# Sparse stages of a 12-stage transformer kernel: next stage's first weight item split between the last two units, and the first two units' outputs taken before the third unit's maximum

## The chip, the cores and the metric

The kernel runs on one core of a Trainium2 chip. The metric is the device time of one execution in microseconds (us). Engines are named as in the profile: PE is TensorE (matmuls; PEld are its weight loads), DVE is VectorE, ACT is ScalarE, POOL is GpSimd, SP is SyncE, which issues the weight transfers. All engines run their own instruction streams and wait for each other on semaphores.

## What is computed

Two blocks, each of depth 2, over 256 tokens of width 1024, in fp32. The first block has feed-forward, a hybrid mixer, cross-attention to a memory and a second feed-forward; the second block, which is where the change is, has a mixer with sparse attention and a squared-relu feed-forward. Cut to the part that matters:

```python
def second_block(x, positions, ...):
    for l in range(DEPTH):                                # DEPTH = 2
        h = rms_norm_2(x, g_pre_mix[l])
        u_pool, q, k, v, iq, ik, iw = split(h @ w_in[l])  # q, k, v: 512 wide, 8 heads of 64
        ...                                               # rotary positions
        a_out = pool_mixer(u_pool, w_pool[l], pool_scale[l])
        b_out = dsa_attention(q, k, v, iq, ik, iw, 64)    # 64 best keys per query by an index score
        mix = concatenate([a_out, b_out]) @ w_out[l]
        x = x + rms_norm_2(mix, g_post_mix[l])
        h = rms_norm_2(x, g_pre_ffn[l])
        f = square(relu(h @ w_ff1[l])) @ w_ff2[l]         # 1024 -> 4096 -> 1024
        x = x + rms_norm_2(f, g_post_ffn[l])
# in dsa_attention, for the chosen keys of each query:
#   s = q . k / 8 ; p = softmax(s) ; o = p @ v
```

## The kernel before

The work is a row of 12 stages, numbered s = 0 to 11: ffn, hybrid, memory, ffn, twice, then sparse, relu, sparse, relu. The two sparse stages are s = 8 and s = 10; each is followed by a relu stage (9 and 11). The order of the work is written out by hand, once for each engine (functions `scalar`, `vector`, `tensor`, `gpsimd`, `sync`); nothing reorders it. On DVE and ACT every instruction waits for the one before it on the same engine.

Weights come in items of 1 MB (mostly 128 x 2048 elements). SP loads item i into one of four `raw` buffers once DVE has finished item i - 4. Each item is then split in two numbers of lower precision that TensorE multiplies: ACT writes the high part (`whi`, or `mhi` where the fourth home is used), DVE the low part, raw minus high (`wlo` or `mlo`), each in two halves of 128 x 1024. `split_to(i, halves)` on either engine advances this splitting up to item i (with `halves=1`, to its first half only), and `take(s, tag, c)` means `split_to` of that item plus AHEAD = 2: two items ahead of the one that PE works on. ACT may write an item's high part only when PE has finished with the item that had the same home (the event `used`). For the first item of a relu stage that older item is `w_out2` number 2. So in a sparse stage `take(s, "w_out2", 2)` is the splitting of the first item of the *next* stage, called `ff1 0` in this text, and `take(s, "w_out2", 3)` that of the second, `ff1 1`.

Activations are split in the same way: PE transposes a tile of 128 tokens (`blocks`), ACT writes the high part into `ahl`, DVE the low part (`halves` on both engines). PE's product with that tile waits for DVE's part.

Attention of a sparse stage is done in four units u = 0 to 3 (tokens tile 0 with head groups 0 and 1, then tile 1 with the same). For each unit PE makes the scores; DVE adds the mask, takes the maximum and negates it (`head(u)`: two additions from PSUM, a reduction, a small multiplication); ACT takes exponentials with their sums (`exps`); PE transposes them (`turn_scores`); ACT, and for units 2 and 3 DVE too, copy them back (`turned`); PE multiplies with the values (`values`); DVE divides by the sums into XN (`out(u)`: a reciprocal and a multiplication). PE transposes XN's half (`blocks`) for the output product `out_part`. `out_part(x, m)` is item x of `w_out2` times tokens tile m: 12 matmuls. PE's order at the end of the stage is `out_part(2,0)`, `turn_scores(2)`, `out_part(2,1)`, `values(2)`, `turn_scores(3)`, `out_part(3,0)`, `values(3)`, `out_part(3,1)` with the last transposition in it, `out_part(0,1)`, `out_part(1,1)` with the transpositions of the next stage's tokens, and then the product that opens the next stage, which begins with `ff1 0`.

At the same place DVE's order is: `turned(2)`, `out(2)`, `turned(3)`, `weigh` and `renew` (which norm tile 0's result and add it to the running X), `out(3)` between them, `halves` of the last tile, then the splitting of `ff1 0` and `ff1 1`, and then the next stage's `halves(s, 0, 0, 0)`, which its first product needs. ACT's is: exponentials of unit 3, `turned(3)`, the squares of tile 0's result (`post_square`), the splitting of `ff1 0`, `halves` of the last tile, `ff1 1`.

Of the kernel before, what the change touches and what calls it, by code (L numbers as in the profile page):

```python
# [32 lines left out]
AHEAD = 2  # L33
# [107 lines left out]
def bm(ap, n):  # L141
    return ap.unsqueeze(1).broadcast_to([ap.shape[0], n, ap.shape[1]])
# [120 lines left out]
def build(nc, A, out):  # L263
    ctx = ExitStack()
    with ctx:
# [178 lines left out]
        number = {x[0]: i for i, x in enumerate(items)}  # L444
# [239 lines left out]
        def scalar(e):  # L684
# [23 lines left out]
            def take(s, tag, c, ahead=AHEAD):  # L708
                split_to(number[s, tag, c] + ahead)
# [142 lines left out]
            def exps(name, l, u, w, P, scale):  # L852
                n, d = (snb, sden) if name == "s" else (nb, den)
                o = 4 * (u if name == "s" else u % 2)
                q.wait_ge(*dve.at(name + "_max", l, u))
                for i in range(4):
                    put(P[u % 2][:, i, 0:w], P[u % 2][:, i, 0:w], ACT.Exp, (name + "_exp", l, u, i), scale=scale,
                        bias=n[:, o + i:o + i + 1], accum_out=d[:, o + i:o + i + 1])
# [149 lines left out]
            def sparse(s):  # L1008
                l = STAGES[s][1]

                def natural(banks, o, name):
                    q.wait_ge(*pe.at(name, l))
                    for m in range(2):
                        put(o[:, m * 512:(m + 1) * 512], PS[:, banks[m], :], ACT.Copy, (name, l) if m else (name, l, 0),
                            scale=r2[:, m:m + 1])

                def heads(o, bank, name):
                    for m in range(2):
                        q.wait_ge(*pe.at(name, l, m))
                        put(o[:, :, m * 128:(m + 1) * 128], PS[:, bank + m, :].rearrange("p (k n) -> p k n", k=4), ACT.Copy,  # L1020
                            (name, l, m))

                def index(m):
                    q.wait_ge(*pe.at("index", l, m))
                    put(RL[m], PS[:, 4:8, :].rearrange("p b (a n) -> p b a n", a=2)[:, :, :, 0:128 * (m + 1)], ACT.Relu,
                        ("index", l, m), scale=0.125 * 8.0 ** -0.5)

                def turned(u):
                    q.wait_ge(*pe.at("s_turned", l, u, 0))
                    put(sPT[u % 2][:, 0:512], PS[:, STURN[u][0], :], ACT.Copy, ("s_pt", l, u))  # L1030

                for m in range(2):
                    q.wait_ge(*pe.at("first", s, m))
                    q.wait_ge(*pool.at("r2", s, m))
                    put(iqk[:, m, 0:292], PS[:, m, 0:292], ACT.Copy, ("iq_first", l, m), scale=r2[:, m:m + 1])
                    put(iqk[:, m, 292:576], PS[:, 4 + m, 0:284], ACT.Copy, ("iq_rest", l, m), scale=r2[:, m:m + 1])
                for m in range(2):
                    put(iw[:, m, :], PS[:, 4 + m, 284:292], ACT.Copy, ("iq", l) if m else ("iw", l), scale=r2[:, m:m + 1])
                for c in range(2):
                    take(s, "q", c)  # L1040
                natural((2, 3), qn, "q")
                heads(iqT, 4, "iqT")
                for c in range(2):
                    take(s, "k", c)
                index(0)
                take(s, "v", 0)
                natural((0, 1), kn, "k")
                index(1)
                q.wait_ge(*dve.at("score", l, 0))
                heads(sqT, 2, "sqT")  # L1050
                take(s, "v", 1)
                heads(skT, 2, "skT")
                take(s, "u", 0)
                natural((0, 1), V, "v")
                exps("s", l, 0, 128, sP, 1.0)
                exps("s", l, 1, 128, sP, 1.0)
                turned(0)
                turned(1)
                take(s, "u", 1)
                take(s, "w_out2", 0)  # L1060
                natural((2, 3), U, "u")
                halves(s + 0.5, 0, 1, TILEBANK[0])
                for a in range(2):
                    q.wait_ge(*pe.at("means", l, a))
                    put(DT[:, a * 512:a * 512 + 512], PS[:, MEANBANK[a], :], ACT.Copy, ("means", l, a))
                exps("s", l, 2, 256, sP, 1.0)
                for a in range(2):
                    q.wait_ge(*pe.at("pooled", l, a))
                    for g in (2 * a, 2 * a + 1):
                        put(ahv[:, g, :], PS[:, POOLBANK[a], (g % 2) * 256:(g % 2) * 256 + 256], ACT.Copy,  # L1070
                            ("pooled", l, g), scale=PSC[:, l * 4 + g:l * 4 + g + 1])
                take(s, "w_out2", 1)
                turned(2)
                exps("s", l, 3, 256, sP, 1.0)
                turned(3)
                post_square(s + 1, 0)
                take(s, "w_out2", 2)
                halves(s + 0.5, 1, 1, TILEBANK[1])
                take(s, "w_out2", 3)

# [6 lines left out]
        def vector(e):  # L1087
# [27 lines left out]
            def split_to(i, halves=2):  # L1115

                while at["split"] < 2 * min(i, len(items) - 1) + halves:
                    n, h = at["split"] // 2, at["split"] % 2
                    at["split"] += 1
                    k, w = items[n][2:4]  # L1120
                    raw, (hi, lo) = raw_of(n), homes[place[n]]
                    c = slice(h * k * w // 2, (h + 1) * k * w // 2)
                    q.wait_ge(*act.at("hi", n, h))
                    tt(lo[:, c], raw[:, c], hi[:, c].bitcast(F32), ALU.subtract, *([("lo", n)] if h else []))

            def take(s, tag, c, ahead=AHEAD):
                split_to(number[s, tag, c] + ahead)
# [54 lines left out]
            def weigh(s, m):  # L1182

                if m == 0:
                    post_weigh(s, m, 0)
                post_var(s, m)
                post_weigh(s, m, 1)
# [378 lines left out]
            def sparse(s):  # L1566
# [26 lines left out]
                def head(u):  # L1593
                    m, g = SUNITS[u]
                    w, b = 128 * (m + 1), SBANK[u]
                    bi = PSC2[:, m * 128:m * 128 + w]
                    q.wait_ge(*pe.at("s_scores", l, u))
                    if u >= 2:
                        q.wait_ge(*pe.at("s_turned", l, u - 2, SUNITS[u - 2][0]))
                    for i in range(2):  # L1600
                        sv = PS[:, b + i, :].rearrange("p (a n) -> p a n", a=2)[:, :, 0:w]
                        stt(sP[u % 2][:, 2 * i:2 * i + 2, 0:w], sv, 0.125, bm(bi, 2), ALU.mult, ALU.add, ("s_shift", l, u, i))
                    o = 4 * u
                    red(smx[:, o:o + 4], sP[u % 2][:, :, 0:w], ALU.max)
                    ts(snb[:, o:o + 4], smx[:, o:o + 4], -1.0, None, ALU.mult, ALU.bypass, ("s_max", l, u))

                def turned(u):
                    q.wait_ge(*pe.at("s_turned", l, u, 1))
                    cp(sPT[u % 2][:, 512:1024], PS[:, STURN[u][1], :], ("s_pt", l, u))

                def out(u):
                    m, g = SUNITS[u]
                    o = 4 * u
                    q.wait_ge(*act.at("s_exp", l, u, 3))
                    rcp(sden[:, o:o + 4], sden[:, o:o + 4])
                    x0 = m * DM + 512 + g * 256

                    q.wait_ge(*pe.at("s_values", l, 1 if u == 0 else u))
                    tt(XN[:, x0:x0 + 256].rearrange("p (a b d) -> p b a d", a=2, b=2),
                       PS[:, SVALUE[u], (u % 2) * 256:(u % 2 + 1) * 256].rearrange("p (b a d) -> p b a d", b=2, a=2),  # L1620
                       bc(sden[:, o:o + 4].rearrange("p (b a) -> p b a", a=2), 64), ALU.mult, ("s_out", l, u))
# [6 lines left out]
                head(0)  # L1628
                head(1)
                select(1)  # L1630
                head(2)
                out(0)
                out(1)
                take(s, "u", 0)
                halves(s + 0.5, 0, 1, TILEBANK[0])
                take(s, "u", 1)
# [6 lines left out]
                head(3)  # L1643
                take(s, "w_out2", 1)
                turned(2)
                out(2)
                turned(3)
                weigh(s + 1, 0)
                out(3)
                renew(s + 1, 0, (0,))  # L1650
                halves(s + 0.5, 1, 1, TILEBANK[1])
                renew(s + 1, 0, (1,))
                take(s, "w_out2", 2)
                take(s, "w_out2", 3)

            for s in range(12):
# [685 lines left out]
```

## Time and profile before

| | |
|---|---|
| time, median of 3 runs | 1870.56 us (1870.31 to 1873.33) |
| profiled execution | 1871.79 us, of which the span from first to last instruction is 1869.7 us |
| granted TensorE clock, mean | 1.000 |
| PE matmuls busy | 1840.9 us, 98% of the span |
| DVE busy | 1314.5 us, 70% |
| ACT busy | 1042.5 us, 56% |
| POOL busy | 216.6 us, 12% |
| DMA | 339.46 MB, mean 182 GB/s |

The profile gives busy times by engine, the waits between engines, and a timeline of each engine. A timeline's row has the start from the span's beginning, the duration, the engine, the line of the helper that issued the instruction, what it writes and reads, the count of merged instructions, and in brackets how long the engine sat idle before it and which engine's result ended that. Since helpers issue nearly everything, most rows have the same few line numbers: 1667 for PE's matmuls, 1672 for its transpositions, 1093 for DVE's two-operand operations, 690 for everything on ACT; one tells them apart by the tile names and by their place.

### The profile page before, as it was taken

What the parts mean: (1) busy time and instruction counts of PE and PEld (TensorE: products, weight loads), DVE (VectorE), ACT (ScalarE), POOL (GpSimd) and SP (SyncE); (2) the same over time, 40 slices, a digit from 0 to 9 for tenths busy, and PEclk for the clock granted to TensorE, in tenths of its full rate; (3) what the DMA queues carried; (4) which work ended last, traced back from release to release, by engine and by line L of the source; (5) the groups of instructions that cost most, each with busy time, mean ns of one, the idle gap of its engine ahead of it and who ended that gap; (6) DMA issues with size and microseconds to landing.
All of it is one profiled execution on the core that took longest, in us unless ns stands there. A gap on an engine that the chain in (4) does not pass through costs nothing.

```text
span 1869.7 us, 27904 instructions
## 1 busy us (share of the span) xinstructions
PE 1840.9 (98%) x10911; PEld 1609.9 (86%) x10911; DVE 1314.5 (70%) x1734; ACT 1042.5 (56%) x1503; POOL 216.6 (12%) x264
## 2 busy tenths in 40 slices
PE   6999999999999999999999999999999999999998
PEld 6888899888888888889998988888888888888887
DVE  5776758777766776676687677666887667787665
ACT  4655545655655565555456566555755545665453
POOL 1010101010100011001021000002201111301110
PEclk9999999999999999999999999999999999999999
DMA  8585663355566556766344536655546654636562
GB/s 288 180 300 188 169 201 121 113 176 174 181 202 203 180 182 233 258 169 223 124 136 136 169 136 225 202 178 168 180 135 205 197 184 164 225 96 210 180 198 73
DMA packets 229971, 339.46 MB, mean 182 GB/s; under 512 B 22278, under 2 KB 178064, under 8 KB 229840
## 3 DMA queue, kind: packets, MB, share of 16 engines
q1 hardware_dynamic: 221968, 307.91, 50.2%
q0 software_dynamic: 7872, 29.78, 4.8%
q8 instruction: 85, 1.39, 0.3%
q14 instruction: 46, 0.38, 0.1%
HBM read 336.62 MB, written 1.05 MB: 181 GB/s over the span
## 4 chain that ended last, share of the span: by engine, by line
PE 90%; DVE 7%; ACT 2%; issue 1%; DMA 1%; DVEq 0%; SPq 0%; ACTq 0%
PE ps L1667 87%; PE ps L1672 3%; DVE wlo L1093 2%; ACT region L690 1%; DVE xn L1093 1%; DVE region L1101 1%; DVE mlo L1093 1%; DMA raw<-ffn_w_gate 1%; DVE xs L1101 1%; ACT whi L690 1%; DVE ahl L1093 0%; DVE hlo L1093 0%; DVE region L1093 0%; DVE region L1590 0%; DVE sm L1588 0%
## 5 line engine op out<-in xcount | busy, mean ns | idle before, releaser
L1093 DVE TENSOR_TENSOR wlo<-raw,whi 128x1024 fp32r<-128x1024 f32 (+2 forms) x458 | 559.5, 1222 | 178.1 <-ACT whi L690 143.6
L690 ACT ACTIVATE whi<-raw 128x1024 fp32r<-128x1024 f32 (+2 forms) x458 | 482.5, 1053 | 66.9 <-PE ps L1667 15.9
L1667 PE MATMUL ps<-ahl,whi 128*128 128x512 f32 (+1 forms) x1920 | 433.4, 353 | 0.2
L1667 PEld LDWEIGHTS ps<-ahl,whi 128*128 128x128 f32 x1920 | 331.2, 190 | 43.1 <-DVE hlo L1093 0.9
L690 ACT ACTIVATE region<-ps 128x512 f32<-128x512 f32 (+2 forms) x260 | 150.2, 578 | 335.8 <-PE ps L1667 251.2
L1667 PE MATMUL ps<-whi,ahl 128*128 128x512 f32 (+2 forms) x1120 | 303.5, 348 | 9.2 <-DVE ahl L1093 8.8
L1667 PE MATMUL ps<-ahl,wlo 128*128 128x256 f32 x1568 | 269.1, 282 | 0.0
L1667 PEld LDWEIGHTS ps<-ahl,wlo 128*128 128x128 f32 x1568 | 233.3, 191 | 11.9
L1667 PEld LDWEIGHTS ps<-whi,ahl 128*128 128x128 f32 x1120 | 197.6, 190 | 35.0 <-DVE ahl L1093 10.9
L1093 DVE TENSOR_TENSOR mlo<-raw,mhi 128x1024 fp32r<-128x1024 f32 x130 | 160.8, 1237 | 49.8 <-ACT mhi L690 40.8
L1667 PE MATMUL ps<-wlo,ahl 128*128 128x512 f32 (+2 forms) x560 | 191.4, 342 | 0.0
L1667 PE MATMUL ps<-whi,hhi 128*128 128x512 f32 x472 | 185.7, 394 | 2.0 <-DVE hlo L1093 2.0
L1667 PE MATMUL ps<-wlo,hhi 128*128 128x512 f32 x472 | 184.3, 390 | 0.0
L1667 PE MATMUL ps<-whi,hlo 128*128 128x512 f32 x472 | 183.8, 389 | 0.0
L531 POOL TENSOR_TENSOR hlo<-region,hhi 128x512 fp32r<-128x512 f32 x62 | 81.1, 1308 | 798.8 <-ACT hhi L690 798.8
L690 ACT ACTIVATE mhi<-raw 128x1024 fp32r<-128x1024 f32 x130 | 137.5, 1058 | 12.9 <-PE ps L1667 5.1
L1667 PE MATMUL ps<-ahl,mhi 128*128 128x512 f32 (+1 forms) x640 | 144.5, 354 | 0.1
L1093 DVE TENSOR_TENSOR region<-region,ps 128x512 f32<-128x512 f32 x102 | 70.1, 688 | 96.3 <-ACT region L690 90.1
L1667 PE MATMUL ps<-region 128*128 128x64 f32 (+5 forms) x928 | 130.1, 327 | 0.0
L690 ACT ACTIVATE hhi<-region 128x512 fp32r<-128x512 f32 x68 | 43.0, 632 | 150.0 <-DVE region L1101 76.6
L1667 PEld LDWEIGHTS ps<-region 128*128 128x128 f32 (+2 forms) x928 | 109.3, 179 | 16.7 <-issue 3.5
L1667 PEld LDWEIGHTS ps<-ahl,mhi 128*128 128x128 f32 x640 | 110.8, 190 | 14.6 <-DVE hlo L1093 0.3
(166 smaller groups left out, 2379.8 us busy)
## 6 DMA issues: line engine op xcount, KB each, us to landing
raw<-w_ff SPq DMA_DIRECT2D x64, 1024.0 KB, 5.4
raw<-ffn_w_gate SPq DMA_DIRECT2D x44, 1024.0 KB, 5.3
raw<-ffn_w_up SPq DMA_DIRECT2D x44, 1024.0 KB, 5.7
raw<-ffn_w_down SPq DMA_DIRECT2D x44, 1024.0 KB, 5.0
raw<-w_in SPq DMA_DIRECT2D x38, 1024.0 KB, 6.1
raw<-w_out SPq DMA_DIRECT2D x16, 1024.0 KB, 4.9
raw<-xa_wk SPq DMA_DIRECT2D x8, 1024.0 KB, 5.2
raw<-xa_wv SPq DMA_DIRECT2D x8, 1024.0 KB, 5.0
```

The lines of the kernel that those rows point to most:

```text
L531: e.tensor_tensor(o, a, b, op).then_inc(*pool.did(*names))
L690: e.activation(o, i, f, **kw).then_inc(*act.did(*names))
L1093: e.tensor_tensor(o, a, b, op).then_inc(*dve.did(*names))
L1101: e.scalar_tensor_tensor(o, a, s, b, op0, op1).then_inc(*dve.did(*names))
L1667: m = e.matmul(o, l, r, start=start, stop=stop)
L1672: m = e.transpose(o, i, CS[0:k, 0:k])
```

## The change

Four edits, all in the sparse stages, in the orders of DVE and ACT. PE's, POOL's and SP's orders are as before.

```diff
@@ scalar: sparse @@
                 take(s, "w_out2", 1)
                 turned(2)
                 exps("s", l, 3, 256, sP, 1.0)
+                take(s, "w_out2", 2)
                 turned(3)
                 post_square(s + 1, 0)
-                take(s, "w_out2", 2)
                 halves(s + 0.5, 1, 1, TILEBANK[1])
                 take(s, "w_out2", 3)
@@ vector: sparse @@
                 head(0)
                 head(1)
                 select(1)
-                head(2)
                 out(0)
                 out(1)
+                head(2)
                 take(s, "u", 0)
                 halves(s + 0.5, 0, 1, TILEBANK[0])
                 take(s, "u", 1)
@@ vector: sparse @@
                 head(3)
                 take(s, "w_out2", 1)
                 turned(2)
+                split_to(number[s, "w_out2", 2] + AHEAD, halves=1)
                 out(2)
                 turned(3)
+                take(s, "w_out2", 2)
                 weigh(s + 1, 0)
                 out(3)
                 renew(s + 1, 0, (0,))
                 halves(s + 0.5, 1, 1, TILEBANK[1])
                 renew(s + 1, 0, (1,))
-                take(s, "w_out2", 2)
                 take(s, "w_out2", 3)
```

On DVE, after the selection of the 64 keys of tile 1 in stage 8 (the `pc` row is its end), the order before (-) and after (+); `small` holds maxima and sums, `xn` rows are `out(0)` and `out(1)`:

```order
 L1097 TENSOR_SCALAR pc<-region 128x256
-L1101 SCALAR_TENSOR_TENSOR region<-ps,pc 128x512 x2
-L1109 TENSOR_REDUCE small<-region 128x4
-L1097 TENSOR_SCALAR small<-small 128x4
 L1113 RECIPROCAL small<-small 128x4
 L1093 TENSOR_TENSOR xn<-ps,small 128x2x2x64
 L1113 RECIPROCAL small<-small 128x4
 L1093 TENSOR_TENSOR xn<-ps,small 128x2x2x64
+L1101 SCALAR_TENSOR_TENSOR region<-ps,pc 128x512 x2
+L1109 TENSOR_REDUCE small<-region 128x4
+L1097 TENSOR_SCALAR small<-small 128x4
 L1093 TENSOR_TENSOR wlo<-raw,whi 128x1024 x2
```

The four instructions of `head(2)` moved behind the four of the two outputs.

On DVE at the end of stage 8, from the last weight item before `turned(2)` on; the `mlo` rows are the halves of `ff1 0`:

```order
 L1093 TENSOR_TENSOR wlo<-raw,whi 128x1024 x2
 L1105 COPY region<-ps 128x512
+L1093 TENSOR_TENSOR mlo<-raw,mhi 128x1024
 L1113 RECIPROCAL small<-small 128x4
 L1093 TENSOR_TENSOR xn<-ps,small 128x2x2x64
 L1105 COPY region<-ps 128x512
+L1093 TENSOR_TENSOR mlo<-raw,mhi 128x1024
 L1093 TENSOR_TENSOR xn<-ps,gv 128x512
 L1097 TENSOR_SCALAR nm<-nm 128x1
```

One half now stands ahead of `out(2)`, the other behind the copy of `turned(3)`; further down, between `renew` and the pair of `ff1 1`, both are gone (in stage 10 the same, with `wlo` in place of `mlo`):

```order
 L1101 SCALAR_TENSOR_TENSOR xs<-xn,nm,xs 128x512
 L1093 TENSOR_TENSOR xn<-xs,gv 128x512
-L1093 TENSOR_TENSOR mlo<-raw,mhi 128x1024 x2
 L1093 TENSOR_TENSOR wlo<-raw,whi 128x1024 x2
 L1093 TENSOR_TENSOR ahl<-ps,ahl 128x4x128
```

What is left behind them is the pair of `ff1 1` and then the next stage's first `halves`.

On ACT in stage 8, from the exponentials of unit 3 on:

```order
 L690 ACTIVATE region,small<-region,small 128x256 x4
-L690 ACTIVATE region<-ps 128x512
-L690 ACTIVATE region,nm<-ps 128x512 x2
-L690 ACTIVATE mhi<-raw 128x1024 x2
+L690 ACTIVATE mhi<-raw 128x1024 x2
+L690 ACTIVATE region<-ps 128x512
+L690 ACTIVATE region,nm<-ps 128x512 x2
 L690 ACTIVATE ahl<-ps 128x4x128
```

The high part of `ff1 0` moved from behind the copy of `turned(3)` and the two squares to ahead of them.

## Rows read from the trace of the kernel before

**Rows 1.** Waits of PE, 1280 to 1400 us: total, times, longest
```profile
PE ps L1667 <- DVE ahl L1093: 1.6, 2, 0.9
```
**Rows 2.** Timeline of PE: start, duration, what, count, idle before
```profile
1377.41 0.39 PE L1667 MATMUL ps<-mhi,ahl 128*128 128x512 f32 x1
...
1394.38 0.39 PE L1667 MATMUL ps<-wlo,ahl 128*128 128x512 f32 x1
1394.61 0.40 PE L1667 MATMUL ps<-whi,ahl 128*128 128x512 f32 x1
1395.90 0.36 PE L1667 MATMUL ps<-mhi,ahl 128*128 128x256 f32 x1 [0.90 <-DVE ahl L1093]
...
1396.93 0.40 PE L1667 MATMUL ps<-mhi,ahl 128*128 128x256 f32 x2
...
1397.29 0.50 PE L1667 MATMUL ps<-mhi,ahl 128*128 128x256 f32 x2
...
1683.92 0.35 PE L1667 MATMUL ps<-whi,ahl 128*128 128x256 f32 x1 [0.90 <-DVE ahl L1093]
```
**Rows 3.** Timeline of PE's weight loads
```profile
1360.58 0.42 PEld L1672 LDWEIGHTS ps<-cs,xn 128*128 128x128 f32 x4 [0.53 <-DVE xn L1093]
...
1363.89 0.19 PEld L1667 LDWEIGHTS ps<-whi,ahl 128*128 128x128 f32 x1 [0.23 <-DVE ahl L1093]
...
1386.09 0.59 PEld L1672 LDWEIGHTS ps<-cs,xn 128*128 128x128 f32 x4
...
1395.87 0.19 PEld L1667 LDWEIGHTS ps<-mhi,ahl 128*128 128x128 f32 x1 [1.31 <-DVE ahl L1093]
```
**Rows 4.** Timeline of DVE, end of stage 8 and start of 9
```profile
1376.86 0.69 DVE L1105 COPY region<-ps 128x512 f32<-128x512 f32 x1
...
1379.70 0.42 DVE L1093 TENSOR_TENSOR xn<-ps,small 128x256 f32<-128x256 f32 x1 [1.94 <-PE ps L1667]
1380.58 0.69 DVE L1105 COPY region<-ps 128x512 f32<-128x512 f32 x1 [0.46 <-PE ps L1672]
1382.75 0.69 DVE L1093 TENSOR_TENSOR xn<-ps,gv 128x512 f32<-128x512 f32 x1 [1.48 <-ACT region L690]
1384.06 0.21 DVE L1097 TENSOR_SCALAR nm<-nm 128x1 f32<-128x1 f32 x1 [0.62 <-ACT region L690]
...
1385.32 0.42 DVE L1093 TENSOR_TENSOR xn<-ps,small 128x256 f32<-128x256 f32 x1
...
1389.82 2.48 DVE L1093 TENSOR_TENSOR mlo<-raw,mhi 128x1024 fp32r<-128x1024 f32 x2
1392.41 2.55 DVE L1093 TENSOR_TENSOR wlo<-raw,whi 128x1024 fp32r<-128x1024 f32 x2
1395.07 0.69 DVE L1093 TENSOR_TENSOR ahl<-ps,ahl 128x512 fp32r<-128x512 f32 x1
```
**Rows 5.** Timeline of ACT, same stretch
```profile
1377.67 0.19 ACT L690 ACTIVATION_READ_ACCUMULATOR region<-region,small 128x1 f32 x1
1380.15 0.60 ACT L690 ACTIVATE region<-ps 128x512 f32<-128x512 f32 x1 [2.29 <-PE ps L1672]
...
1384.12 2.15 ACT L690 ACTIVATE mhi<-raw 128x1024 fp32r<-128x1024 f32 x2
...
1392.52 0.60 ACT L690 ACTIVATE ahl<-ps 128x512 fp32r<-128x512 f32 x1 [1.97 <-PE ps L1672]
...
1394.34 0.60 ACT L690 ACTIVATE ahl<-ps 128x512 fp32r<-128x512 f32 x1 [0.44 <-PE ps L1672]
```
**Rows 6.** Timeline of DVE, middle of stage 8
```profile
1355.93 1.42 DVE L1101 SCALAR_TENSOR_TENSOR region<-ps,pc 128x512 f32<-128x512 f32 x2
...
1363.15 0.69 DVE L1093 TENSOR_TENSOR ahl<-ps,ahl 128x512 fp32r<-128x512 f32 x1
```
**Rows 7.** Timeline of SP, stage 8; page: weight transfers, KB each, us to landing
```profile
1363.07 54.59 SPq L501 DMA_DIRECT2D raw<-w_ff  x9
```
```profile
raw<-w_ff SPq DMA_DIRECT2D x64, 1024.0 KB, 5.4
```

## The prediction

> **What bounds the kernel now.** I read the page's busy times first: PE is busy for 1840.9 of 1869.7 us, 98%, as the small table has it. PE's own order is untouched, so an edit on DVE or ACT can only give back a stretch in which PE waits for them, or make a new one. The second view is therefore PE's waits around the first sparse stage and its end [rows 1]: 1.6 us in two waits, both for DVE's low part of the activations (`ahl`), the longest 0.9. The third is PE's timeline, for where that wait stands: at 1395.90, the first matmul of stage 9, whose left operand is `mhi`, that is `ff1 0`; stage 11 has its twin at 1683.92, also 0.90 [rows 2]. The other wait of [rows 1] lies ahead of the edited code, at the start of stage 8, and is left alone.
>
> What is DVE doing while PE waits? The fourth view, DVE's timeline, shows the low part at 1395.07, ended 0.69 later at 1395.76, with PE following 0.14 behind. Straight ahead of it stand two pairs of weight halves, `mlo` (`ff1 0`, 2.48 us) from 1389.82 and `wlo` (`ff1 1`, 2.55) from 1392.41 [rows 4]. ACT had written the high part of the same activations at 1392.52 + 0.60 = 1393.12 [rows 5]. So for 1.95 us the low part could have been made and was queued behind weights. A little earlier DVE sits idle for 1.94, 0.46, 1.48 and 0.62 us [rows 4].
>
> **Part 1: the halves of ff1 0 move forward.** First whether they fit.
>
> ACT: its exponentials end at 1377.67 + 0.19 = 1377.86, and it then idles 2.29 us until 1380.15, when it copies unit 3 [rows 5]. Its pair of high halves costs 2.15 [rows 5]. They may start when `w_out2` 2 is used, which is PE's last matmul of `out_part(2,1)`, 1377.41 + 0.39 = 1377.80 [rows 2]: no wait to speak of. The item itself is in `raw` long since: the first transfer of this stretch of `w_ff` was issued at 1363.07, and such a transfer takes 5.4 us, so 1368.5 [rows 7]. With a few hundredths between instructions the pair runs from about 1377.93 to 1380.10, and the copy at 1380.15 starts 0 to 0.05 late. What is behind it on ACT, the squares, waits for PE anyway.
>
> DVE: the copy of `turned(2)` ends at 1377.55. The first low half waits for ACT's first high half (1377.93 + 1.07 = 1379.00), takes 1.24 (half of 2.48), ends about 1380.27. Queued behind this wait are the reciprocal, the multiplication of `out(2)` and the copy of unit 3. The multiplication, before at 1379.70, comes at about 1380.57, and the copy, before at 1380.58, at about 1381.02: 0.9 and 0.45 us late. Nobody on PE wants `out(2)` at once (its reader is the transposition at 1386.09 [rows 3]); the copy ends at 1381.71, while PE still has `out_part(3,0)` to do before `values(3)`. The second half then takes 1381.80 to 1383.05, in the 1.48 us of idleness before 1382.75, and pushes that instruction by 0.35 to 1383.10. It ends at 1383.80, and the next, at 1384.06, was waiting for ACT with 0.62 of idleness, so it starts on time [rows 4]. From there everything to 1389.78 is as before. The margin: 0.25 us at 1384.06, and behind it another 0.35, since `out(3)` ends at 1385.32 + 0.42 = 1385.74 [rows 4] and PE loads it at 1386.09 [rows 3]. Some 0.6 us in all, and the moved work costs nothing on the path.
>
> What it gives: at 1389.82 the `mlo` pair is gone and DVE goes to `ff1 1`, whose pair ends near 1392.4 instead of 1394.96. ACT's high part at 1393.12 becomes what is late next, and DVE's low part runs from 1393.17 to 1393.86 in place of 1395.76. PE's last matmul before the wait starts at 1394.61 and has 512 columns; it and the one before (1394.38) are 0.23 us apart, so the first of stage 9 would start at 1394.84 instead of 1395.90: 1.06 us, a little more than the 0.90 that the row calls idle and less than the 1.31 of its weight load [rows 2, 3]. Then there is a small second one: in the run of matmuls of 256 columns a pair takes 0.40, but 0.50 at 1397.29 [rows 2], where the second half of the activations is first read. It also goes, since ACT has its high part at 1394.34 + 0.60 = 1394.94 [rows 5] and DVE's low part can follow by 1395.7, while PE would want it at 1394.84 + 1.44 = 1396.3. So 0.10 more, 1.16 us for a sparse stage. Behind that, the chain over tile 1 starts from ACT and DVE work that is earlier by more than 1.16, or from PE, so it moves along, and stages 9 and 11 show PE without a wait in the stretches behind these. Price between bounds: at least the 0.90 of the row if a matmul there starts no sooner, at most the 1.31 of the weight load plus 0.10 = 1.41. I take 1.16.
>
> There is a rule that speaks against the edit. On ACT and DVE each instruction waits for its predecessor, so a half at the head that waits for `used` or for its high part holds back all behind it; in this trace DVE idled 1.94 us for one such wait [rows 4]. The Trainium skill says the same of the queues (TensorE: Matmul & The Clock Gate, the table at its head and "Architectural detail: the array is 16x 32x32, not 1x 128x128"): ACT's and DVE's queues are strictly first in, first out, while PE may pull weight loads ahead. By that rule nothing passes the two halves, and the sum stands only while they fit, which is the rival "slower" below. The second half of the rule, loads pulled ahead, agrees with the trace as far as the load at 1395.87 waited longer (1.31) than its matmul (0.90) [rows 2, 3].
>
> SP: the load of the item four behind `ff1 0` waits for its low part and so is issued about 9 us earlier (1383.1 instead of 1392.3). PE waited for no weights there, so this gives nothing and needs nothing.
>
> **Part 2: out(0) and out(1) ahead of head(2).** It moves two reciprocals and two multiplications forward past four instructions. PE's transposition of them waited 0.53 us at 1360.58 [rows 3]; that wait goes. But DVE is busy without a gap worth naming from 1355.93 to the low part that starts at 1363.15 and ends at 1363.84 [rows 6], and PE's weight load at 1363.89 waits for just that, with 0.23 of idleness [rows 3]. The same instructions stand between, in another order, so it ends at 1363.84 again. PE gets there up to 0.5 earlier and waits that much longer. I price it at 0, bounds +0.1 to -0.3 for a stage: small gaps between dependent small instructions can fall otherwise, and DVE is what decides. `head(2)` ends under 2 us later, and ACT's exponentials of unit 2 stand behind copies of what PE makes after its transposition at 1360.58, which is cover.
>
> **Sum.** Two sparse stages at 1.16 is 2.32 us. The profiled execution took 1871.79, so it would take 1869.47. That execution is 1.23 above the median of the runs shown, 1870.56; on the median the forecast is 1868.24, say 1868.2.
>
> **Rivals.**
> - *The wait is filled, but something else holds PE there* (the low part made in time, then PE stopped by the weights of `ff1 1` or by the second half of the activations). For it: DVE's order is dense there, and `ff1 1` also waits for ACT. Against: by the times above each has 0.6 us or more of margin. It would give about half, 1.2 us: 1869.4. With both gains lost, 1870.6.
> - *Part 2 pays too.* If DVE's stretch to 1363.84 shortens or PE profits from earlier transpositions elsewhere: 0.5 us a stage on top, 1867.2. Against it is the row at 1363.89.
> - *Slower.* The first low half holds `out(2)`, the copy of unit 3 and the post-norm chain. It decides once it is more than 0.6 us late beyond my times, for instance if ACT's high half started late; from there PE loses one for one at 1386.09. To lose on balance it must be over 1.76 us late. Were it late by a whole transfer, 5.4 us [rows 7], the stage would lose 5.4 - 0.6 - 1.16 = 3.6, and the kernel 7.3: 1877.9. Against it: the item lands 9 us before ACT now wants it, and the other release, at 1377.80, is a matmul that PE reaches without help from the moved work.
> - *The change does not do what it says*: the DVE halves land elsewhere. The order shows them where the diff puts them; no chance worth a number of its own.
>
> **How the numbers follow.** Forecast (1.8 to 2.8 us gained) 0.68; gain partly or wholly refilled 0.17; part 2 pays too 0.11; slower 0.04. A measurement of this kernel tells about 0.2% from no change, 3.7 us: faster means below 1866.8, slower above 1874.3. The forecast lies inside. Below 1866.8 I see part of the rival in which part 2 pays, and a forecast that the median of a few runs moves by 1.4 us (the three shown span 3): 0.13. Above 1874.3: 0.04. The rest, 0.83, is within. The range is 1866.5 to 1870.7: from the upper bounds of both parts (1.41 + 0.3 twice, 1867.1, and a little for the runs) to no gain at all.
>
> **What would show it.** Right: no wait of 0.9 us at the first `ff1 0` matmul of stages 9 and 11, each span from the last `out_part` to it shorter by 1.06; DVE's first low half at about 1379.0 with a wait for ACT before it, the second before the post-norm multiplication; that one's successor still at 1384.06; the low part of the activations at about 1393.2, waiting for ACT. For part 2: the wait of 0.53 gone, the one for `ahl` after it grown by as much. Wrong: PE's transposition at 1386.09 later, a wait at `values(3)`, or a new PE wait in the first 15 us of stage 9.

## The result and the profile after

The changed kernel takes 1868.77 us (median of 21 runs, 1867.67 to 1871.5) where the kernel before, timed beside it, takes 1871.36 (21 runs): a ratio of 0.9986, 95% interval 0.9980 to 0.9992, that is 2.6 us faster. Forecast were 1868.2 us and a gain of 2.3 us. The gain is small, below the 3.7 us that the prediction took as what a measurement tells, but with 21 runs each the interval excludes 1: it stands for a gain of 1.5 to 3.7 us.

The profiled execution has a span of 1867.6 us, 2.1 less than before. That understates the edit. PE's first transposition came 0.8 us later in this execution, before any changed instruction, and the delay was still 0.85 us at A in stage 8. So I measure inside the stage, between PE's transpositions, which all kernels of this study have in the same order. For stage 8 in the trace of before they start at: A 1349.83 (exponentials of units 0 and 1), B 1360.58 (the outputs of units 0 and 1), C 1386.31 (the last tile), D 1393.71 (the second of the two transpositions of the next stage's first tokens), E 1408.15 (the scales, near the end of stage 9's first product). The changed kernel's rows are

```profile
1350.68 1.04 PE L1673 MATMUL ps<-cs,region 128*128 128x128 f32 x8
...
1361.24 0.66 PE L1673 MATMUL ps<-cs,xn 128*128 128x128 f32 x4
...
1386.93 0.60 PE L1673 MATMUL ps<-cs,xn 128*128 128x128 f32 x4
...
1394.31 0.60 PE L1673 MATMUL ps<-cs,xn 128*128 128x128 f32 x4
...
1407.44 0.38 PE L1673 MATMUL ps<-cs,nm 128*128 128x128 f32 x2
```

The table is worked out from such starts (us).

| | A to B, stage 8 / 10 | B to C | C to D | D to E | A to E, both stages |
|---|---|---|---|---|---|
| before | 10.75 / 10.58 | 25.73 / 25.72 | 7.40 / 7.40 | 14.44 / 14.44 | 116.46 |
| changed | 10.56 / 10.56 | 25.69 / 25.70 | 7.38 / 7.38 | 13.13 / 13.13 | 113.53 |

The two stretches together are 2.93 us shorter: 2.62 of it is D to E (1.31 us in each), where [rows 2] had the wait, 0.21 is A to B, and 0.10 is B to D. PE's timeline of the changed kernel, from the last `out_part` into the first product:

```profile
1393.86 0.39 PE L1668 MATMUL ps<-wlo,ahl 128*128 128x512 f32 x1
...
1395.21 0.40 PE L1668 MATMUL ps<-whi,ahl 128*128 128x512 f32 x1
1395.45 0.28 PE L1668 MATMUL ps<-mhi,ahl 128*128 128x256 f32 x1
1395.57 0.28 PE L1668 MATMUL ps<-mlo,ahl 128*128 128x256 f32 x1
...
1396.75 0.40 PE L1668 MATMUL ps<-mhi,ahl 128*128 128x256 f32 x2
...
1399.39 0.60 PE L1673 MATMUL ps<-cs,xn 128*128 128x128 f32 x4
```

The first `mhi` matmul follows at 0.24 us, where it was 1.29 later before (1394.61 to 1395.90), and it has no bracket: PE waits for nothing. All pairs are 0.40 long, none 0.50 as in [rows 2].

DVE in the same stretch, the lines that answer to [rows 4]:

```profile
1377.48 0.69 DVE L1105 COPY region<-ps 128x512 f32<-128x512 f32 x1
1379.69 1.23 DVE L1093 TENSOR_TENSOR mlo<-raw,mhi 128x1024 fp32r<-128x1024 f32 x1 [1.52 <-ACT mhi L690]
...
1381.76 0.69 DVE L1105 COPY region<-ps 128x512 f32<-128x512 f32 x1
1382.56 1.23 DVE L1093 TENSOR_TENSOR mlo<-raw,mhi 128x1024 fp32r<-128x1024 f32 x1
1383.91 0.69 DVE L1093 TENSOR_TENSOR xn<-ps,gv 128x512 f32<-128x512 f32 x1
1384.71 0.21 DVE L1097 TENSOR_SCALAR nm<-nm 128x1 f32<-128x1 f32 x1
...
1388.20 0.69 DVE L1093 TENSOR_TENSOR ahl<-ps,ahl 128x512 fp32r<-128x512 f32 x1
...
1390.51 2.55 DVE L1093 TENSOR_TENSOR wlo<-raw,whi 128x1024 fp32r<-128x1024 f32 x2
1393.76 0.69 DVE L1093 TENSOR_TENSOR ahl<-ps,ahl 128x512 fp32r<-128x512 f32 x1 [0.69 <-ACT ahl L690]
```

All times here are 0.62 later than on the scale of [rows 4], by PE's transposition C. The halves are where the forecast put them: the first at 1379.07 on the old scale (forecast 1379.00), the second at 1381.94 (1381.80). The low part of the new tile starts at 1393.14 (forecast 1393.17) and now waits for ACT instead of standing behind weights. Note also what has vanished: the post-norm multiplication at 1383.91 and its successor at 1384.71 have no idle time before them any more, and neither has the low part of the last tile at 1388.20. From 1379.69 to there DVE is one unbroken chain.

ACT answers to [rows 5]:

```profile
1378.60 2.15 ACT L690 ACTIVATE mhi<-raw 128x1024 fp32r<-128x1024 f32 x2
1380.84 0.60 ACT L690 ACTIVATE region<-ps 128x512 f32<-128x512 f32 x1
...
1393.13 0.60 ACT L690 ACTIVATE ahl<-ps 128x512 fp32r<-128x512 f32 x1 [1.96 <-PE ps L1673]
```

The pair fills the old idleness of 2.29 us, and the copy of unit 3 is 0.07 us late by the old scale.

Part 2 shows in DVE's middle stretch (compare [rows 6]) and in the weight loads (compare [rows 3]):

```profile
1358.27 1.42 DVE L1101 SCALAR_TENSOR_TENSOR region<-ps,pc 128x512 f32<-128x512 f32 x2
...
1363.76 0.69 DVE L1093 TENSOR_TENSOR ahl<-ps,ahl 128x512 fp32r<-128x512 f32 x1
```
```profile
1361.23 0.42 PEld L1673 LDWEIGHTS ps<-cs,xn 128*128 128x128 f32 x4 [0.33 <-DVE small L1097]
...
1388.95 0.19 PEld L1668 LDWEIGHTS ps<-whi,ahl 128*128 128x128 f32 x1 [0.46 <-DVE ahl L1093]
```

PE's load of the outputs has 0.33 of idleness left of 0.53, and the load of `out_part(0,0)` behind it, which waited 0.23, is no longer among the rows with a wait. The bracket names the end of `head(2)`, but that is only what ended last before the load. The transposition needs `out(1)`, and that had been done for 3 us; what PE was still at was its own matmuls of unit 3's scores:

```profile
1357.81 0.42 DVE L1093 TENSOR_TENSOR xn<-ps,small 128x256 f32<-128x256 f32 x1
...
1360.17 1.13 PE L1668 MATMUL ps<-region 64*128 64x256 f32 x8
```

From A to B is 10.56 us in both stages now. So the part of the 0.53 that DVE caused was about 0.2.

The row at 1388.95 is the wait for the last tile's low part. It was there in the kernel before as well, and DVE had a little idleness before that part:

```profile
1388.33 0.19 PEld L1667 LDWEIGHTS ps<-whi,ahl 128*128 128x128 f32 x1 [0.45 <-DVE ahl L1093]
```
```profile
1387.58 0.69 DVE L1093 TENSOR_TENSOR ahl<-ps,ahl 128x512 fp32r<-128x512 f32 x1 [0.18 <-ACT ahl L690]
```

### The profile page after: what moved, and what is told of

It is laid out like the page before. It is cut to its first block, busy times and chain, and to the rows that moved or that the text cites. A ratio compares the mean times of both kernels' runs of the same rounds, so it can differ in the third digit from the quotient of the medians.

```text
span 1867.6 us, 27904 instructions
## 1 busy us (share of the span) xinstructions
PE 1840.6 (99%) x10911; PEld 1611.5 (86%) x10911; DVE 1314.9 (70%) x1734; ACT 1042.3 (56%) x1503; POOL 216.3 (12%) x264
## 3 DMA queue, kind: packets, MB, share of 16 engines
HBM read 336.62 MB, written 1.05 MB: 181 GB/s over the span
## 4 chain that ended last, share of the span: by engine, by line
PE 92%; DVE 5%; ACT 2%; DMA 1%; issue 1%; DVEq 0%; SPq 0%; ACTq 0%
PE ps L1668 89%; PE ps L1673 3%; DVE wlo L1093 2%; ACT region L690 1%; DVE xn L1093 1%; DMA raw<-ffn_w_gate 1%; DVE region L1101 1%; DVE mlo L1093 1%; ACT whi L690 1%; DVE xs L1101 0%; DVE hlo L1093 0%; DVE ahl L1093 0%; DVE region L1093 0%; ACT hhi L690 0%; ACT mhi L690 0%
```

## The experiments

In each, the ratio is to the kernel before timed beside it, and A to E is the sum of both stages, to be compared with 116.46 (before) and 113.53 (changed).

**Halves only.** `out(0)` and `out(1)` put back behind `head(2)`:

```diff
-                out(0)
-                out(1)
                 head(2)
+                out(0)
+                out(1)
```

> Only the halves of ff1 0 moved (ACT and DVE), the two outputs left behind head(2). Theory: nearly all of the change is here. PE's stretch from the last transposition of stage 8 to the first of the next product loses about 1.3 us a stage (1.06 of the wait, the rest small waits behind it), in all 2.6 us against the kernel before; DVE's stretch from the key selection to the low part of tile 0 stays as long as before (7.61 and 7.44 us in the trace before). Rival (the two edits need each other): less than 1.5 us in all.

Measured: 1869.64 us, ratio 0.9988 (0.9979 to 0.9997). A to E 113.89, so 2.57 less than before; D to E 13.13 in both stages, as in the changed kernel. A to B 10.77 and 10.59, as before. The theory holds: the moved halves are nearly all of the gain.

**Outputs first only.** The kernel before with `out(0)`, `out(1)` ahead of `head(2)`, the halves untouched.

> Only out(0) and out(1) ahead of head(2). Theory as predicted: 0, since DVE decides at the low part of tile 0. What the changed kernel's trace says instead: DVE's stretch from the selection to that low part is 7.37 us in both sparse stages, where it was 7.61 and 7.44, so PE gains what DVE's stretch loses, 0.24 and 0.07 us, 0.3 in all. Rival (part 2 pays by itself as much as its wait): 0.5 us a stage, 1.0 in all.

Measured: 1871.35 us, ratio 0.9999 (0.9990 to 1.0008): a run cannot tell it from nothing. The trace can: A to E 116.21, 0.25 less, nearly all in A to B (10.56 in both stages). DVE shows where it comes from. The kernel before and, second, this one, from the second reciprocal:

```profile
1359.72 0.18 DVE L1113 RECIPROCAL small<-small 128x4 f32<-128x4 f32 x1
1360.10 0.42 DVE L1093 TENSOR_TENSOR xn<-ps,small 128x256 f32<-128x256 f32 x1 [0.21 <-DVE small L1113]
```
```profile
1356.21 0.18 DVE L1113 RECIPROCAL small<-small 128x4 f32<-128x4 f32 x1
1356.42 0.42 DVE L1093 TENSOR_TENSOR xn<-ps,small 128x256 f32<-128x256 f32 x1
```

The multiplication starts 0.20 behind its reciprocal's end in the first, 0.03 in the second. That gap stands at this place in stage 8 in all three traces with the old order (before, halves only, and ACT only, below) and in none of the nine with the new one; in stage 10 the old order does not have it. The rest of what DVE's stretch lost in stage 8 (7.61 to 7.37 us, from the selection's last instruction to the low part), 0.07, is shorter gaps elsewhere. Stage 10 is the control: its old order has no such gap, DVE's stretch went from 7.44 to 7.37 us, and PE gained 0.02 from A to B and 0.04 in all. So moving the outputs forward gained next to nothing by itself; what PE gained in stage 8 is what the gap had cost. The two parts together should give 2.57 + 0.25 = 2.82; the changed kernel has 2.93.

**One half.** DVE's second half of `ff1 0` left at its old place:

```diff
                 turned(3)
-                take(s, "w_out2", 2)
                 weigh(s + 1, 0)
 ...
                 renew(s + 1, 0, (1,))
+                take(s, "w_out2", 2)
                 take(s, "w_out2", 3)
```

> The changed kernel, but DVE's second half of ff1 0 left where it was before; only the first half goes ahead of out(2). Theory (PE waits for the low part of the activations behind whatever stands before it, until ACT's high part decides): with one half left, the low part starts 1.24 us earlier than before, at 1393.8 on the time scale of before, and ends at 1394.5, just before PE's weight load at 1394.6. So the large wait of 1.06 still goes, but the small ones behind it come back in part: 1.0 to 1.2 us a stage instead of 1.3. Rival (a half counts as a half): 0.65 us a stage.

Measured: 1869.32 us, ratio 0.9987 (0.9978 to 0.9996). D to E 13.20 in both stages: a gain of 1.24 from the first half, and 0.07 more from the second. A wait behind two pieces of 1.24 us is not halved when one leaves: the one was enough to put the low part ahead of PE. Expected were 1.0 to 1.2, a little low; the rival's 0.65 is out.

**Unsplit.** Both halves ahead of `out(2)`:

```diff
-                split_to(number[s, "w_out2", 2] + AHEAD, halves=1)
+                take(s, "w_out2", 2)
                 out(2)
                 turned(3)
-                take(s, "w_out2", 2)
```

> The changed kernel, but both halves of ff1 0 on DVE ahead of out(2), so not split between the units. Theory (0.6 us of margin): the copy of unit 3 ends 1.24 + 0.1 us later than in the changed kernel, on the changed kernel's time scale at about 1383.8, where PE's weight load for values(3) starts at about 1383.5: PE loses 0.2 to 0.4 us a stage there; behind it nothing else, so the kernel is 0.4 to 0.8 us slower than the changed one. Rival (splitting does not matter): same within 0.1 us. Rival (splitting is what pays): 2.5 us slower.

Measured: 1869.29 us, ratio 0.9988 (0.9980 to 0.9997); A to E 114.00, 0.47 more than the changed kernel. B to C is 25.90 and 25.93 where the changed kernel has 25.69 and 25.70, and nothing else differs by more than 0.02. So splitting the item between the units is worth 0.2 us a stage, at the low end of what was expected; runs cannot tell it.

**ACT only.** The kernel before with ACT's `take` moved and nothing on DVE.

> The kernel before, with only ACT's part of the move: its high halves of ff1 0 come ahead of the copy of unit 3, DVE's order is that of before. Theory (DVE's queue makes the wait, not ACT's): DVE's low part of the activations starts where it did, the waits of 0.90 us at the first matmul of stages 9 and 11 stay, the time is that of before within 0.2 us. Rival (ACT's late high half was what held DVE): the wait goes and the kernel gains 1 us or more a stage.

Measured: 1871.99 us, ratio 1.0002 (0.9993 to 1.0011), A to E 116.51, D to E 14.44 and 14.46. DVE's order makes the wait; ACT's move only allows DVE's.

**DVE only.** The changed kernel with ACT's `take` back behind `post_square`.

> The changed kernel, with ACT's high halves left where they were. This is the forecast's slower rival made real: DVE's first low half must wait for ACT's high half, which comes 6.2 us later than in the changed kernel, and out(2), the copy of unit 3 and the norm chain are queued behind it. Theory (0.6 us of margin at the end, about 1.2 us at values(3), then one for one): DVE's first half starts at 1385.2 on the time scale of before, the copy of unit 3 ends at about 1387.9, where PE wants it at 1382.9, so PE waits about 5 us at values(3) in stages 8 and 10; gained back is the 1.2 to 1.3 us of the later wait. Net 3.5 to 4 us slower a stage, 7 to 8 us in all against before. Rival (PE has other work to cover it): under 2 us.

Measured: 1885.2 us (4 runs), ratio 1.0071 (1.0056 to 1.0086): 13.5 us slower, nearly twice what was expected. DVE, then PE:

```profile
1385.34 1.23 DVE L1093 TENSOR_TENSOR mlo<-raw,mhi 128x1024 fp32r<-128x1024 f32 x1 [7.66 <-ACT mhi L690]
...
1387.40 0.69 DVE L1105 COPY region<-ps 128x512 f32<-128x512 f32 x1
```
```profile
1383.04 0.39 PE L1668 MATMUL ps<-whi,ahl 128*128 128x512 f32 x1
1388.24 3.64 PE L1668 MATMUL ps<-region 128*128 128x64 f32 x16 [4.82 <-DVE region L1105]
1391.65 0.77 PE L1668 MATMUL ps<-whi,ahl 128*128 128x512 f32 x1
1392.22 0.63 PE L1668 MATMUL ps<-wlo,ahl 128*128 128x512 f32 x1
```

The wait is as forecast: DVE's half at 1385.34, the copy ended at 1388.09, PE 4.82 us idle at `values(3)`. But the 16 matmuls of `values(3)` then take 3.64 us instead of 1.89 (changed kernel), and those behind them 0.63 instead of 0.39. The stage by stretches (columns: length, busy us and instructions of PE, PEld, DVE, ACT, POOL, then the granted clock, DMA share, GB/s):

```profile
1384.00:1388.00 4.00, 0.00 (x0) 0.00 (x0) 2.42 (x4) 2.27 (x4) 0.00 (x0) 0.92 0.00 0
1388.00:1390.00 2.00, 1.75 (x9) 1.79 (x9) 1.79 (x3) 0.00 (x0) 0.00 (x0) 0.50 0.00 0
1390.00:1392.00 2.00, 2.00 (x10) 2.00 (x10) 1.38 (x5) 0.00 (x0) 0.56 (x1) 0.50 0.65 141
1392.00:1394.00 2.00, 2.00 (x6) 1.52 (x6) 1.78 (x3) 0.00 (x0) 0.00 (x0) 0.50 1.04 368
1394.00:1396.00 2.00, 2.00 (x12) 1.53 (x10) 0.47 (x2) 0.60 (x1) 0.00 (x0) 0.96 0.05 15
```

The granted clock falls in the last part of the wait (a mean of 0.92 over the first row), is 0.50, the lower level of 1.2 GHz, until about 1394, and then full again. B to C grew by 33.53 - 25.69 = 7.84 us against the changed kernel: 5.20 - 0.23 = 4.97 from the last matmul before the wait to the first after it, and 6.04 - 3.17 = 2.87 from there to C, which is the clock.

In stage 10 PE is idle as long (4.81, the 16 matmuls 3.65 long), but the lower level lasts longer, from the wait until about 1691, past C at 1688.85:

```profile
1688.00:1690.00 2.00, 2.00 (x8) 1.70 (x7) 0.51 (x1) 0.06 (x1) 0.00 (x0) 0.50 0.26 93
1690.00:1692.00 2.00, 2.00 (x8) 1.53 (x8) 1.40 (x2) 0.54 (x2) 0.00 (x0) 0.72 0.00 0
```

There B to C grew by 7.92 and C to D by 0.78, so the same wait cost 7.8 us in one stage and 8.7 in the other. The two waits alone, 4.97 and 4.96, less the 2.93 of the changed kernel, would be 7.0 us against the kernel before, as expected; the clock is the rest.

The Trainium skill (TensorE: Matmul & The Clock Gate, "Part 1: The HAM clock gate") says that an idle TensorE falls to its lower clock and has to earn the higher one back; the trace agrees, with the 0.50 above while PE was busy again.

**Extra half.** The changed kernel, with the first half of `ff1 0` computed once more between the copy of unit 3 and the second half:

```diff
                 out(2)
                 turned(3)
+                again(number[s, "w_out2", 2] + AHEAD)   # lo[:, first half] = raw - hi
                 take(s, "w_out2", 2)
```

> The changed kernel with one more half on DVE: the first low half of ff1 0 is computed a second time, between the copy of unit 3 and the second half (1.24 us with its gap about 1.3; the result is the same). Theory: it eats the margin and what is over moves PE one for one. In the changed kernel's trace the norm's multiplication had ended 0.1 us before its successor started, out(3) ends at 1386.39 and PE's load of it is at about 1386.7. With 1.3 us more, less the 0.1 and the 0.3, PE loses about 0.9 to 1.0 us a stage, 1.8 to 2.0 us against the changed kernel. Rival (DVE's idle time of 70% busy covers it): 0. Rival (a DVE instruction on this stretch always counts in full): 2.6 us.

Measured: 1871.29 us, ratio 0.9997 (0.9989 to 1.0006). A to E 115.96, 2.43 more than the changed kernel: 1.21 a stage. Neither the expected 0.9 to 1.0 nor the rival's 1.3 is met, and the rival is nearer. B to C grew by 0.78 and 0.76, about as the theory has it (PE waits for `out(3)`), but C to D by 0.44 and 0.45, which it did not have. PE:

```profile
1387.19 0.66 PE L1679 MATMUL ps<-cs,xn 128*128 128x128 f32 x4 [0.61 <-DVE xn L1093]
...
1389.65 0.50 PE L1674 MATMUL ps<-whi,ahl 128*128 128x512 f32 x1 [0.41 <-DVE ahl L1093]
```

**Extra half, tile first.** To find what the second wait is:

```diff
                 out(3)
-                renew(s + 1, 0, (0,))
                 halves(s + 0.5, 1, 1, TILEBANK[1])
+                renew(s + 1, 0, (0,))
                 renew(s + 1, 0, (1,))
```

> The kernel with the extra half, with one more edit on DVE: the low part of the last tile (`halves` of 8.5 and 10.5) goes ahead of the first half of `renew`. The extra half alone cost 1.21 us a stage, of which 0.78 at the last transposition (PE waits for out(3)) and 0.44 behind it, up to out_part(0,1). New theory: that 0.44 is DVE's queue again, since the low part stood behind renew's two instructions, which the extra half had made later; taken out of it, the stretch from the last transposition to the second of the next tokens returns from 7.82 to 7.38 us, while the 0.78 stay: 0.43 us a stage back. Rival (the 0.44 is ACT's or PE's own, or the slowed weight loads after a wait): the stretch stays at 7.8.

Measured (a single run, 1871.69 us, so the trace alone counts): C to D 7.43 and 7.48 instead of 7.82 and 7.83, and B to C as it was. So that part of the theory holds: the low part stood behind `renew`. But the 0.4 us do not come back. D to E goes from 13.13 to 13.61 and 13.56, and A to E ends at 116.15. DVE after the swap:

```profile
1388.52 0.69 DVE L1093 TENSOR_TENSOR ahl<-ps,ahl 128x512 fp32r<-128x512 f32 x1 [1.38 <-ACT ahl L690]
...
1392.48 2.55 DVE L1093 TENSOR_TENSOR wlo<-raw,whi 128x1024 fp32r<-128x1024 f32 x2
1395.14 0.69 DVE L1093 TENSOR_TENSOR ahl<-ps,ahl 128x512 fp32r<-128x512 f32 x1
```

DVE now idles 1.38 us for the last tile, everything behind it is late, and the low part of the next tile has no idle time before it: it is behind `ff1 1` again, and PE waits there, as its weight load shows:

```profile
1395.89 0.19 PEld L1674 LDWEIGHTS ps<-mhi,ahl 128*128 128x128 f32 x1 [0.41 <-DVE ahl L1093]
```

The wait moved on to the next place that needs the same engine.

**Relu end.** The same idea where a wait of the same kind is left. At the end of stage 9 the changed kernel has

```profile
1567.43 0.47 PE L1668 MATMUL ps<-whi,hhi 128*128 128x512 f32 x1 [0.97 <-DVE hlo L1093]
```

and DVE had done both halves of the next stage's first item before it. The edit is `halves=1` in that `split_to`.

> The changed kernel with the same idea at another place: at the end of stage 9 (relu) PE waits 0.97 us for DVE's low part of the last hidden tile, which stands behind both halves of the next stage's first item. Here only the first half goes ahead of it, the second behind. Theory: the wait goes, worth 1.0 to 1.2 us at that place; but the second half now stands before the post-norm chain, which had 0.29 us of idleness, so up to 1 us can come back at the transpositions that open stage 10: 0 to 1.2 us faster than the changed kernel, I say 0.5. Rival (the chain is what counts): no gain.

Measured: 1867.91 us, ratio 0.9983 (0.9974 to 0.9992). The wait is gone; from stage 9's first transposed hidden tile (1410.84 in the changed kernel) to the first transposition of stage 10 takes 162.35 instead of 162.98 us, 0.63 less; one of 0.46 appears for the post-norm chain:

```profile
1572.45 0.65 PE L1673 MATMUL ps<-cs,xn 128*128 128x128 f32 x4 [0.46 <-DVE xn L1093]
```

It has the lowest median here, but its interval and that of the changed kernel overlap. 0.36 us was lost again near the start of stage 11, where PE's first transposition of the hidden tiles now waits 0.24 us for DVE; all ends has the same, and why is open.

**All ends.** The same `halves=1` at the ends of the four ffn stages besides.

> The kernel with the edit at the relu stage's end, and the same at the ends of the four ffn stages, where PE waits 0.34 us (three stages) for the same kind of low part. Theory: 0.5 us at each of the three waits goes, but the post-norm chain behind has no idle time there (0.1 us), so it is 1.2 us later and PE waits at the next tokens' transpositions: no gain or a loss of up to 0.7 us a stage, 0 to 2 us in all. Rival (a wait removed is a gain): 1.5 us faster than without it.

Measured: 1869.34 us, ratio 0.9990 (0.9981 to 0.9999), 1.4 us slower than relu end alone. The three waits of 0.34 went, and three longer ones came at the next tokens' transpositions, such as

```profile
839.38 0.66 PE L1673 MATMUL ps<-cs,xn 128*128 128x128 f32 x4 [0.90 <-DVE xn L1093]
```

There the post-norm chain on DVE had only 0.49 us of idleness in the changed kernel, for a half of over 1.2 us; at the end of stage 9 it was 0.29 + 0.61 = 0.90 us:

```profile
202.51 0.22 DVE L1101 SCALAR_TENSOR_TENSOR nm<-nm 128x1 f32<-128x1 f32 x1 [0.49 <-ACT region L690]
```

## Why the prediction was right, and where it was not

*Where the wait is and what makes it.* Right. Halves only keeps 2.57 of 2.93 us; ACT only keeps nothing. One reading beside it does not hold: that the load waited longer than its matmul (1.31 against 0.90) only says that the load before it had ended earlier, not that loads run ahead. What shows that is the same load in the changed kernel, which starts at 1395.22, 0.23 us ahead of its matmul and just behind the start of the matmul before.

*Do the halves fit.* Right for the place and times of both, within 0.15 us, and in that they cost PE nothing. SP's next load into the buffer of `ff1 0` was issued at 1383.81 instead of 1392.33 and, as forecast, gave nothing that the trace shows.

Wrong for the margin, which was given as 0.25 us at the norm's successor and 0.35 at the transposition, 0.6 in all. The first 0.25 was used up by the edit itself: with gaps of 0.1 us between DVE's instructions the successor, which was to start on time at 1384.06, started at 1384.09 with no idleness before it. At the transposition the size came out near: the extra half made `out(3)` end 1.26 us later (36.97 instead of 35.71 behind A) and PE's transposition start 0.78 later, so 0.48 was absorbed. But the transposition was not the reader that decides. The low part of the last tile stood right behind the first half of `renew`, PE already waited 0.45 us for it in the kernel before, and DVE had 0.18 us of idleness there, which the edit filled. This reader the prediction did not follow. With it the extra half cost 1.21 us, nearly all of itself: the margin was about nothing, not 0.6. That the time did not suffer is luck as far as this reader goes: the edit was closer to its edge than the prediction said.

*The gain at the wait.* 1.16 forecast, 1.31 measured in each stage, within the bounds of 0.90 to 1.41. The term of the large wait was right (1.06 forecast; 1394.61 to 1395.90 before and 1395.21 to 1395.45 after give 1.29 - 0.24 = 1.05), and so was the 0.10 of the second half. Missed were two small ones. After the wait the second matmul came 0.20 behind the first (1395.90, 1396.10), without it 0.12 (1395.45, 1395.57): the restart cost 0.08 beyond the wait. And the transposition of tile 1 before, 0.66 long, is 0.60 in the changed kernel's row at 1399.39: another 0.06 us, with no bracket; that it was a wait for DVE is likely and not shown. The second matmul after the wait, before:

```profile
1396.10 0.28 PE L1667 MATMUL ps<-mlo,ahl 128*128 128x256 f32 x1
```

*Part 2.* The forecast was 0 with bounds of +0.1 to -0.3 us a stage; measured were -0.19 and -0.02 from A to B, inside the bounds. Of its two signs neither came: the idleness of 0.53 at the transposition's load did not go but fell to 0.33, and the wait for `ahl` behind it did not grow but went. Two steps failed. The 0.53 was read as waiting for DVE, while 0.33 of it stays with the outputs done 3 us before. And "so it ends at 1363.84 again" did not hold: the same instructions took 7.37 us where they had taken 7.61 in stage 8 and 7.44 in stage 10. That DVE decides was right in stage 8: counted from A, PE now starts its load for `out_part(0,0)` at 13.83 us (1364.51), the old low part was done only at 14.01, and the new one is done 0.06 before that load. In stage 10, where PE gained 0.02, the two had come out together before.

*The rivals.* "Something else holds PE there" did not come: after the change the stretch D to E has no PE wait. "Part 2 pays too" was to give 0.5 us a stage; the outputs alone gave 0.25 in the two together. "Slower" had the right mechanism but neither point nor price: the run DVE only shows the wait at `values(3)`, not at the transposition, and it is not one for one, since after 4.8 us of idleness the lower clock adds 2.9 us in stage 8 and 3.7 in stage 10.

*The sum.* 2.32 forecast; 2.93 in the traces, 2.6 in the runs. The 0.61 between forecast and traces is 0.30 at the wait, 0.21 from A to B and 0.10 from B to D. The runs' interval of 1.5 to 3.7 us holds both figures, so that the median lies only 0.6 us from the forecast is no finer proof: by the runs alone the single terms cannot be told, and the division among them rests on one trace of each kernel and on the stages 8 and 10 agreeing.

## What to carry to other kernels

When an engine that is always busy waits once for a small result, look at what its maker did just before: here 5 us of weight splitting that nobody needed yet stood ahead of a 0.7 us instruction. Move such work into idle time of the same queue, and only so much as that idleness holds; one piece of it may do nearly all (here 1.24 of 1.31 us). Then follow every later reader of that queue, not only the nearest, before you call the rest margin: with the idleness filled, each further microsecond counted almost in full.

## What the hardware did that I had not expected

- A wait of 4.8 us on PE cost 7.8 us in stage 8 and 8.7 in stage 10, because the granted clock was 0.50 for some 6 and 8 us after it; the same 16 matmuls took 3.64 instead of 1.89 us. The waits of 1 us and less in these stages left it at 1.00.
- After the wait of 0.90 us PE's second matmul came 0.20 us behind the first instead of 0.12.
- In stage 8 the old order had a gap of 0.20 us between a reciprocal and the multiplication behind it, in three traces of three, and stage 10 with the same instructions had 0.03. Why is open.
